# Two blocks on one core: gate chunks moved into the latent inverse, and a final norm by tokens

## The reference

```python
def first_block(...):                      # twice, then a final rmsnorm
    z = rmsnorm(h, norm1[i]) @ w_in[i]     # pool part, q, k, v
    h = h + concat(pool_out, attn_out) @ w_out[i]
    h = h + square(relu(rmsnorm(h, norm2[i]) @ w_up[i])) @ w_down[i]
    h = h + sigmoid(rmsnorm(h, norm3[i]) @ w_gate[i]) * (p[i] @ w_ple[i])

def second_block(...):
    mod = silu(c) @ w_mod + b_mod          # sh1, sc1, g1, sh2, sc2, g2
    h = modulate(x, norm1_g, sh1, sc1)
    qkv, z, ba, sc_p, fn_u = split_cols(h @ w_in, IN_SIZES)
    # gated delta rule over chunks, two directions, the latent scan starts from
    # the context's state; per chunk t_inv = (I + strictly lower part)^-1
    gates = sigmoid(h @ w_gate + b_gate)   # three branches
    merged = gates[0] * y_dn + gates[1] * y_sc + gates[2] * y_fn
    x = x + g1 * (merged @ w_o)
    x = x + g2 * swiglu(modulate(x, norm2_g, sh2, sc2), w_ffn_in, w_ffn_out)
    return rmsnorm_2(x, final_g)           # swiglu: (silu(a) * b) @ w_ffn_out
```

## Time and profile before

| | |
|---|---|
| median of 3 runs | 1266.12 us (1266.11 to 1269.02) |
| profiled execution | 1265.56 us |
| its span | 1263.8 us |
| granted TensorE clock, mean | 0.997 of full |
| TensorE busy | 97% |
| VectorE, ScalarE, GpSimd busy | 71%, 51%, 8% |
| latent delta with its fills, about | 778 to 921 us |
| gates and outputs of three branches | from 928 us |
| last ffn matmul | 1246.5 us |

### The profile page before, as it was taken

How to read it: one execution, slowest core, us unless ns; L and a number is a source line. 1 busy time by engine, 2 the same in 40 slices (tenths; PEclk the granted TensorE clock), 3 DMA queues, 4 the chain that set the end, 5 groups by cost and what they waited for, 6 DMA issues and landing times.

```text
span 1263.8 us, 20995 instructions
## 1 busy us (share of the span) xinstructions
PE 1221.8 (97%) x8494; PEld 1110.8 (88%) x8494; DVE 897.0 (71%) x1284; ACT 650.3 (51%) x994; POOL 96.9 (8%) x84
## 2 busy tenths in 40 slices
PE   8999999999999999999999999979899999999997
PEld 7889899998999889999999989878789998888886
DVE  6887777777888378766657866786476776666665
ACT  6574544446657366454453665542354555344443
POOL 1230000000024020000000000261100000000000
PEclk9999999999999999999999999999999999999999
DMA  9626677666753443655646755332125566655530
GB/s 323 204 88 204 206 244 246 227 222 192 263 175 117 150 135 117 193 174 185 199 150 218 227 174 151 116 100 68 34 97 171 179 230 218 202 181 190 200 133 34
DMA packets 160782, 219.19 MB, mean 173 GB/s; under 512 B 5712, under 2 KB 135598, under 8 KB 160558
## 3 DMA queue, kind: packets, MB, share of 16 engines
q1 hardware_dynamic: 158962, 214.45, 52.3%
q10 hardware_dynamic: 1724, 3.39, 0.7%
HBM read 215.99 MB, written 1.05 MB: 172 GB/s over the span
## 4 chain that ended last, share of the span: by engine, by line
PE 81%; DVE 7%; issue 3%; ACT 3%; DMA 2%; DVEq 1%; ACTq 1%; SPq 1%; POOL 1%; POOLq 1%
PE bank L557 18%; PE bank L559 17%; PE bank L558 17%; PE bank L606 10%; PE bank L608 5%; PE bank L652 2%; DVE w_lo L548 2%; PE bank L918 2%; PE bank L906 1%; PE bank L1481 1%; DMA w_raw<-in_w_in 1%; DMA arena<-arena 1%; DVE arena L1282 1%; PE bank L935 1%; SPq L2949 1%
## 5 line engine op out<-in xcount | busy, mean ns | idle before, releaser
L548 DVE TENSOR_TENSOR w_lo<-w_raw,w_hi 128x1024 fp32r<-128x1024 f32 (+1 forms) x350 | 421.8, 1246 | 56.1 <-ACT w_hi L539 44.7
L539 ACT ACTIVATE w_hi<-w_raw 128x1024 fp32r<-128x1024 f32 (+1 forms) x350 | 350.1, 1041 | 118.3 <-PE bank L559 57.5
L557 PE MATMUL bank<-act_parts,w_hi 128*128 128x256 f32 x1200 | 345.4, 288 | 9.5 <-DVE w_lo L548 7.3
L558 PE MATMUL bank<-act_parts,w_hi 128*128 128x256 f32 x1200 | 340.0, 283 | 0.0
L559 PE MATMUL bank<-act_parts,w_lo 128*128 128x256 f32 x1200 | 340.0, 283 | 0.0
L557 PEld LDWEIGHTS bank<-act_parts,w_hi 128*128 128x128 f32 x1200 | 230.5, 192 | 19.4 <-issue 13.8
L558 PEld LDWEIGHTS bank<-act_parts,w_hi 128*128 128x128 f32 x1200 | 230.8, 192 | 0.7 <-issue 0.2
L559 PEld LDWEIGHTS bank<-act_parts,w_lo 128*128 128x128 f32 x1200 | 230.6, 192 | 0.0
L606 PE MATMUL bank<-act_parts,w_hi 128*128 128x512 f32 x544 | 191.1, 396 | 1.5 <-DVE act_parts L2297 1.4
L608 PE MATMUL bank<-act_parts,w_lo 128*128 128x256 f32 x544 | 151.3, 278 | 0.0
L557 PE MATMUL bank<-w_hi,side_hi 128*128 128x512 f32 (+1 forms) x392 | 149.5, 381 | 0.0
(11 more groups left out here) (345 smaller groups left out, 1625.7 us busy)
## 6 DMA issues: line engine op xcount, KB each, us to landing
w_raw<-in_w_in SPq DMA_DIRECT2D x39, 1024.0 KB, 5.7
w_raw<-in_w_up SPq DMA_DIRECT2D x32, 1024.0 KB, 6.0
w_raw<-in_w_down SPq DMA_DIRECT2D x32, 1024.0 KB, 4.9
w_raw<-in_w_ffn_in SPq DMA_DIRECT2D x22, 1024.0 KB, 5.2
w_raw<-in_w_gate SPq DMA_DIRECT2D x20, 1024.0 KB, 5.2
w_raw<-in_w_mod SPq DMA_DIRECT2D x32, 512.0 KB, 4.0
w_raw<-in_w_ffn_out SPq DMA_DIRECT2D x11, 1024.0 KB, 5.4
w_raw<-in_w_out SPq DMA_DIRECT2D x8, 1024.0 KB, 5.7
```

The source lines that it names most:

```text
L539: nc.scalar.activation(whi[:, slot, 0:n], raw[:, st.slot(name), n * half:n * (half + 1)], ACT.Copy).then_inc(hi_ready, 1)
L548: nc.vector.tensor_tensor(wlo[:, slot, 0:n], raw[:, st.slot(name), n * half:n * (half + 1)], whi[:, slot, 0:n].bitcast(F32), ALU.subtract) ...
L557: nc.tensor.matmul(o, ahi, bhi, start=start, stop=False, skip_group_check=True)
L558: nc.tensor.matmul(o, ahi, blo, start=False, stop=False, skip_group_check=True)
```

## The change

The latent delta gets 48 units instead of 40: the first two gate chunks of the first branch (ga0, ga1) are projected there in the three-matmul form, into a new buffer first_gates. The units are placed anew: 6 instead of 8 at norm, 2 at a new point x00 between the two transposes of x0 and 1 at x0, one more per level at t, and one each at u1, u3 and s0. The load of ScalarE's exp and ln tables moves behind the first two units. The sibling parts for n = 1 go from GpSimd to VectorE, behind T3. final_norm goes to the four gate chunks of the second branch, two tiles each. Modulation terms move by one or more steps in both layers, and sum_squares(2) goes from behind up chunk 2 to before the relu of up chunk 3.

The ending is by tokens: h is transposed to tokens at the start of the ffn (`h_by_tokens`), the gate g2 is made as a row on all partitions by a matmul with a column of ones at every 32nd partition (`quad`), the rows b_mod and final_g are loaded onto all partitions behind chunk post 24, and no output chunk follows step j = 9. Behind step 10 come output chunk 8 and then chunks 9 and 10 together in four quarters, each complete for 128 tokens and 512 columns.

```diff
-SSQ2_AT = 3
+SSQ2_AT = 4
...
-        "lat": dict(ba=8, norm=8, T0=2, T1=2, T2=2, T3=2, P=2, x0=2, end=1,
-                    **{f"{w}{lv}": 1 for w in "zx" for lv in range(1, LEVELS)})}
+        "lat": dict(ba=8, norm=6, T0=2, T1=2, T2=2, T3=2, P=2, x00=2, x0=1, u1=1, u3=1, s0=1, end=1,
+                    **{f"{w}{lv}": 1 for w in "zxt" for lv in range(1, LEVELS)})}
-LAT_FILL = ["fn0", "fn1"] + [f"sc{c}" for c in range(6)] + ["z0", "z1"]
+LAT_FILL = ["fn0", "fn1"] + [f"sc{c}" for c in range(6)] + ["z0", "z1", "ga0", "ga1"]
...
+NFF = FF2 // 256
+OUTS_AFTER = [[]] + [[j - 1] for j in range(1, NFF - 2)] + [[], [NFF - 3, NFF - 2, NFF - 1]]
+ROWS_AT = 24
...
-for i, at in enumerate([11, 12, up_at(1)] + [up_at(j) for j in range(3, UPS)]):
+for i, at in enumerate([10, 11, 12, up_at(2)] + [up_at(j) for j in range(4, UPS)]):
...
-for i, at in enumerate([up_at(j) for j in range(3, UPS)] + [down_at(j) for j in (12, 13, 14)]):
+for i, at in enumerate([up_at(j) for j in range(4, UPS)] + [down_at(j) for j in (11, 12, 13, 14)]):
...
+        def project_quarters(pe, names, parts, ready, quarter_done):
+            for t in range(TT):
+                tok = slice(P * t, P * (t + 1))
+                for n in range(2):
+                    w = slice(512 * n, 512 * (n + 1))
+                    for i, name in enumerate(names):
+                        if t == n == 0:
+                            ready(i)
+                        hi, lo = parts[i]
+                        for half in range(2):
+                            slot = st.piece(name, half)
+                            if t == n == 0:
+                                pe.wait_ge(lo_ready, st.pieces(name, half))
+                            mm = three(pe, ps[2 * n + t][:, :], hi[half][:, tok], lo[half][:, tok],
+                                       whi[:, slot, w], wlo[:, slot, w], start=False,
+                                       stop=i == len(names) - 1 and half == 1)
+                    mm.then_inc(quarter_done, 1)
...
             if lat:
+                fill("ba", 2)
+                ln_exp_tables()
                 fill("ba")
...
+                if lat:
+                    dve.wait_ge(*told("T", 1))
...
+            if lat:
+                sibling_parts(1)
             fill("P")
             for n in range(TT):
+                if n:
+                    fill("x00")
                 b = W(f"x0{n}")
...
-            for n in range(TT if lat else 0):
+            for n in range(1 if lat else 0):
                 pool.wait_ge(*told("A", 2 * n + 2))
...
+                if j >= 10:
+                    full(nc.tensor.matmul(ps[b][:, :], col("quad").broadcast_to([P, P]), rows_of(j), start=True, stop=True), b)
+                    return
...
+            h_by_tokens(0, 0, 0)
+            h_by_tokens(0, 1, 1)
+            h_by_tokens(1, 0, 2)
             mod_chunk(22, lambda: 3)
...
+            project_quarters(pe, [("post", l), ("post", l + 1)], [ff_parts(nff - 2), ff_parts(nff - 1)],
+                             lambda i: pe.wait_ge(S("ff_act"), nff - 1 + i), S("ffo_quarter"))
...
+            for t in range(TT):
+                for n in range(2):
+                    act.wait_ge(S("y_steps"), 4 * t + 2 * n + 1)
+                    of = slice(512 * n, 512 * (n + 1))
+                    nc.scalar.activation(pre_x.rearrange("p k t -> p (k t)")[:, of], y_rows[:, t, of],
+                                         ACT.Square, accum_out=(tok_part, tok_sum)[n][:, t:t + 1])
+                    act.drain()
...
+                nc.scalar.activation(tok_sum[:, t:t + 1], tok_sum[:, t:t + 1], ACT.Ln, scale=1.0 / D,
+                                     bias=tok_part[:, t:t + 1])
+                act.drain()
+                nc.scalar.activation(tok_rstd2[:, t:t + 1], tok_sum[:, t:t + 1], ACT.Exp, scale=-0.5)
+                act.drain().then_inc(S("post_rstd"), 1)
...
-                if i == 4:
-                    final_norm()
...
+                    if n == 1:
+                        final_norm(c)
...
+            for t in range(TT):
+                for n in range(2):
+                    of = slice(512 * n, 512 * (n + 1))
+                    dve.wait_ge(S("ffo_quarter"), 2 * t + n + 1)
+                    v.tensor_tensor(ff_out[:, t, of], ps[2 * n + t][:, :], gate_row[:, of], ALU.mult)
+                    dve.drain()
+                    v.tensor_tensor(y_rows[:, t, of], y_rows[:, t, of], ff_out[:, t, of], ALU.add)
+                    dve.drain().then_inc(S("y_steps"), 1)
+                    v.tensor_tensor(ff_out[:, t, of], y_rows[:, t, of], final_row[:, of], ALU.mult)
+                    dve.drain().then_inc(S("y_steps"), 1)
+                dve.wait_ge(S("post_rstd"), 4 + t)
+                v.tensor_scalar(ff_out[:, t, 512:D], ff_out[:, t, 512:D], tok_rstd2[:, t:t + 1], None, ALU.mult)
...
+                if name == ("post", ROWS_AT):
+                    sp.wait_ge(S("o_done"), 1)
+                    for to, first in ((b_mod_row, V["b_mod_2"] + 40), (final_row, V["final_g_2"])):
+                        row = a["vec_rows"][first:first + KT, :]
+                        sp.dma_start(to, bass.AP(row.tensor, row.offset, [[0, P], [1, D]])).then_inc(S("row_landed"), 16)
...
+            for t in range(TT):
+                for n, said in enumerate(("y_act", "y_dve")):
+                    of = slice(512 * n, 512 * (n + 1))
+                    sp.wait_ge(S(said), t + 1)
+                    sp.dma_start(y[:, t, of], ff_out[:, t, of]).then_inc(S("stored"), 16)
```

More of the change, by code:

```diff
@@ L241, in filler, with norm_share @@
     return fill
+def norm_share(part, i):
+    n = 4 if part == "lat" else 2
+    return FILL[part]["norm"] * (i + 1) // n - FILL[part]["norm"] * i // n
 def heads(b):
@@ L1198, in dve_delta @@
                     S("lat_qn" if lat and i < 2 else "dn_kn"), 1)
[L1199 removed]
+                fill("norm", norm_share(part, i))
             fill("norm")
@@ L1461, in two_blocks, with gate_of @@
         pool_w = sb("pool_blocks", [P, 2, P])
+        first_gates = sb("first_gates", [P, 4, T])
+        def gate_of(n, k, m):
+            return first_gates[:, k:k + m, :] if n == 0 and k < 4 else gate[:, k:k + m, :]
         two_k = lambda g, i: g.rearrange("p a b -> p (a b)")[:, 1024 * i:1024 * (i + 1)].rearrange(
@@ L1803, in _, with h_by_tokens @@
             sum_tiles(C("norm2"), pre_x, "sq_tiles", 4, 2)
+            def h_by_tokens(t, half, bank):
+                b = banks.claim(pe, f"h_tok{t}{half}", bank)
+                for i in range(4):
+                    mm = tr(ps[b][:, P * i:P * (i + 1)], h[:, 4 * half + i, P * t:P * (t + 1)])
+                full(mm, b)
+            h_by_tokens(0, 0, 0)
+            h_by_tokens(0, 1, 1)
+            h_by_tokens(1, 0, 2)
             mod_chunk(22, lambda: 3)
@@ L2174, in lat_copy @@
                         act.drain().then_inc(S("sc_act"), 1)
+                elif name == "ga":
+                    free(nc.scalar.activation(first_gates[:, two, :], pair(b), ACT.Copy), b)
                 else:
@@ L2246, in _ @@
                 nxt(l)
+                if j < 2:
+                    for t, half in (((0, 0), (0, 1), (1, 0)), ((1, 1),))[j]:
+                        b = W(f"h_tok{t}{half}")
+                        free(nc.scalar.activation(y_rows[:, t, 512 * half:512 * (half + 1)], ps[b][:, :], ACT.Copy), b)
+                    act.drain().then_inc(S("h_tok"), 1)
                 act.wait_ge(S("ff_sum"), j + 1)
```

152 lines of the change are left out of this document (65 added, 87 removed).

## The result

The changed kernel takes 1249.09 us (median of 4 runs, 1248.58 to 1250.52) against 1266.11 for the kernel before (1265.82 to 1269.02): ratio 0.9862, 95% interval 0.9845 to 0.9879. Repeated on another chip the ratio was 0.9881 (0.9866 to 0.9896), the median 1251.88. The forecast was 1247.0 with a range of 1243.5 to 1251.5: 2.1 us too low, and inside the range. The repetition stands near the range's upper end (1251.0 by its ratio). The execution that was profiled took 1249.47, span 1247.7, so 16.1 us less than before's 1263.8.

The account below looks back on a forecast made before the run. TensorE's matmul queue, busy 97% of the span, was taken as the bound. Terms -11.2 + 0.6 + 0.3 - 1.4 + 1.5 - 8.9 = -19.1 gave 1246.5 from 1265.56 profiled, forecast 1247.0 us as median, range 1243.5 to 1251.5.

Parts of the forecast that it names:

- 1: Gate stage: two of four gate chunks, 5.6 us each, leave it, -11.2 us.
- 3: Entry to the branch stage: first gates' sigmoids stand ahead of ScalarE's split for the first fn_out chunk, +0.3 us (0 to 1.5).
- 2: Latent delta: shorter VectorE chain against added units on TensorE, +0.6 us, bounds -2 to +7.8.
- 4: Layers: moving a modulation term and the sum of squares removes two TensorE stalls, -1.4 us (0 to -1.6).
- 5: Mid stream: f32 matmuls for modulation columns and 16 new transposes of h, +1.5 us (0.8 to 2.6).
- 6: Ending: last ffn output in four quarters shortens the stretch behind the last matmul, -8.9 us (-10 to -6).
- C: Inverse levels don't hide the units and waits on X updates return: 7.8 instead of 0.6, 1254.2 us; chance 0.06.
- F: The units only push the delta out, by their full 11.2 instead of 0.6: 1257.6 us; chance 0.03.
- Rival B: Delta's rounds: each of four GpSimd query products blocks VectorE for 1.1 us: +4.0, 1251.0 us; chance 0.15.
- Rival E: Two new row loads crawl and hold back weights at the second branch's gates; slower than before, 1272 at 45 us; chance 0.02.
- Rival D: The ending is 3 us slower, by short ScalarE operations with drains or four stores: 1250.0 us; chance 0.07.
- Rival A: Latent delta: VectorE's chain gets shorter still, delta -2, in all 1244.4 us; chance 0.12.

Follow-up runs that it names:

- GpSimd late: The changed kernel with GpSimd's query, key and value products of the latent delta held until VectorE has made both x0 updates: 1246.09 us, ratio 0.9835.
- its own run: The kernel before with only the new ending (gate row, rows of h, quarters, norm by tokens, four stores): 1259.68 us, ratio 0.9939.
- the pair of late runs: The changed kernel with GpSimd's products held until both x0 updates, with new and with old layer places of terms and sum_squares(2): 1246.09 and 1248.28 us.
- sibling_gpsimd: The changed kernel with sibling_parts(1) back on GpSimd, as in the kernel before: 1244.81 us, ratio 0.9820.
- sibling_late: The changed kernel with sibling_parts(1) back on GpSimd and its products held behind the first level's z products: 1244.47 us, ratio 0.9823.

## Why the prediction was right, and where it was off

The sum was -19.1 and came out as -16.1 in span, 3.0 short. That the medians miss by 2.1 only is chance: before's median lay 0.56 above its profiled execution, the changed kernel's 0.38 below. By terms, before's profile against the changed kernel's:

| term | forecast | measured |
|---|---|---|
| 1, 3 two gate chunks leave, entry to the branch stage | -10.9 | -11.31 |
| 2 latent delta | +0.6 | +5.09 (0.5 with GpSimd late) |
| 4 layers, and the start of the delta | -1.4 | -2.93 |
| 5, 6 middle and ending | -7.4 | -6.95 (7.7 by its own run) |

**1** was the simplest and holds to 0.1 us, with nothing in the measured row for **3**, which had +0.3 (0 to 1.5): TensorE is busy for all of the gate stage's window, 98.74 of 98.74 us. The 1.09 us ahead of the norm product lie in the delta's window, and before had them too.

**2 is the term that was mis-sized.** The step that failed is the pair "those two are the worst of them, about -1.2" and "GpSimd's query products now fall beside the rounds: +0.35". Measured, all that runs on VectorE beside GpSimd up to the second X update costs 4.57 us more than without it. The prediction did see that GpSimd, freed of a sibling part, starts its query products early. It stopped there: behind them on GpSimd's queue stand four key products and then values and keys in turn, and they moved forward with them, out of the cover of the levels and onto the last round, sibling_parts(1) and the splits ahead of the X updates. They made 3.21 of the 4.57. The queries made 1.36. The credit of 1.2 for splits freed of their neighbour was the opposite of what happened: one neighbour left, and a longer one came.

With GpSimd late term 2 is +0.5 (132.59 against 132.07), so the rest of the working stood: a level at 8.97 us (forecast 8.9), hardly a wait behind an update (one of 1.3 in place of ten), the rivals C and F refuted. The move of the sibling part costs 1.3 us net; the prediction had +2.8 - 1.2 = 1.6.

**Rival B** was the right direction and almost the right amount, 1251.0, with another place: it gave each of four query products 1.1 us of blocking, while they took 1.36 together and products that it didn't name took the rest. So part of the forecast's nearness is luck: term 2 was 4.5 us short, and the layers with the start of the delta gave 1.5 us more than they had been given.

**4.** The stalls at 131.5 and 144.0 are gone, as said, and the pair of late runs puts the layer at -1.9, where the forecast had -1.4 and a bound of -1.6. The listed holes (0.40 and 1.01) are smaller than what they cost, as the prediction itself had noted for the inverse and not applied here. Of the rest, 0.4 us is the table load (forecast inside the 0.6), 0.35 the start-up, where executions differ by 1 us, and 0.3 lies in the layers behind.

**5.** Up to the second half of the first ffn chunk the middle gave +0.58 (36.40 us from the end of the gates before, 36.98 after), and the four transposes in the open are 0.43 more: 1.0 for 1.5. What is left, about 1.2, is for the most part a slower pace of the same matmuls in the ffn chunks, told below, so the row of terms 5 and 6 came out at -6.95. Rival E, loads that crawl, is refuted: no wait for a load at the second branch's gates. The last ffn piece was waited for 0.37 us (forecast 0.35).

**6.** From the last matmul's end 7.35 us, for 16.93: -9.6, and -9.2 with the wait of 0.37, against a forecast of -8.9. Rival D's 3 us are refuted, but its sign was there: VectorE was still on the third quarter when TensorE's last matmul ended at 1240.35. It began the last quarter at 1240.90, 0.55 us behind that end, where it had followed the second quarter's last matmul (end 1234.91) by 0.04. The prediction had 0.65 at this place, so it cost nothing against the forecast.

**Rival A** would have needed a delta 2 us shorter than before; none of the versions reached it, the best was 0.8 below (131.27).

## What to carry to other kernels

When work leaves an engine's queue, everything behind it on that queue moves forward: list all of it, to the end of the stage, and look at what each piece then runs beside, not only at the first. If VectorE sets the pace somewhere, hold GpSimd's work back behind it by one wait, as long as there is cover later; here this was worth 3.4 us of 1249 by the ratios (4.6 in the delta), and 6 us, clock included, to the half of the change that it belonged to. And a listed wait of TensorE can cost a few tenths more than its figure (0.40 and 1.01 listed, 1.9 in the pair of late runs), which decides between forecasts when the waits are short.

## What the runs showed of the hardware

**VectorE and GpSimd.** Clearly longer beside GpSimd were only VectorE's operations with both inputs in SBUF: 0.68 to 1.53, 0.69 to 1.37, 1.13 to 1.70, a split from 1.23 to as much as 2.29. Those that read a bank were not in the changed kernel (X updates 1.05 and 1.09 beside it, 1.06 and 1.09 without); the first X update took 1.20 to 1.24 us in three profiles where it ran beside GpSimd's third sibling operation (before, sibling_gpsimd, sibling_late), which stays open. GpSimd pays as well: its four key products took 6.64 us here, and 4.04 in the kernel before, where they ran at 849.30. The Trainium skill (SBUF — State Buffer, "SBUF: two separate sides") says that a VectorE operation with two SBUF inputs and a GpSimd operation that reads SBUF take one port pair in turn, each for its whole length; the trace agrees on which operations suffer, but for those 0.1 us, and adds what it comes to over a stretch: 0.30 to 1.06 us for each of seven.

**Two levels of the clock inside one stretch of work.** TensorE's granted clock fell from 2.4 to 1.2 GHz behind waits for w_lo between 825 and 840 us in most of the profiles, and a second time at about 842 in three of the four profiles with GpSimd's products as early as in the changed kernel, and in none of the seven in which they are later. The length of the wait doesn't settle it: the changed kernel waited 4.09 and 2.95 us in one execution and 4.09 and 2.96 in the other, and from 840 to 850 us the clock was 1.00 and 0.86. If the waits set it off, which is not shown, fewer waits give back more than their length in some executions.

**Two paces at one granted clock.** Thirty-two pairs of matmuls, those of the two input chunks of one ffn step, began at 1084.49 and the next product at 1095.80 in the changed kernel, 11.31 us:

```profile
1084.49 0.40 PE L615 MATMUL bank<-act_parts,w_hi 128*128 128x512 f32 x1
...
1095.80 0.40 PE L566 MATMUL bank<-w_hi,side_hi 128*128 128x512 f32 x1
```

In the kernel before, the same work went from 1092.32 to 1103.41, 11.09 us:

```profile
1092.32 0.40 PE L606 MATMUL bank<-act_parts,w_hi 128*128 128x512 f32 x1
...
1103.41 0.40 PE L557 MATMUL bank<-w_hi,side_hi 128*128 128x512 f32 x1
```

That is 353 and 347 ns for a pair of a 512- and a 256-column matmul, both at a granted clock of 1.00. Other profiles hold the slow pace for all of the ffn, or for a part that begins and ends elsewhere, the same kernel's repetition too. Over the ffn stage, 352 pairs, it comes to 2 us. What sets it stays open; it limits what a single pair of profiles can say of a microsecond.

**The read-out of an accumulator** (ACTIVATION_READ_ACCUMULATOR) is an instruction of its own on ScalarE, 0.19 us behind each square.
